# A two-block transformer kernel on one core: order of the first loads, place of the modulation's columns, and layout of SBUF

## The reference

```python
cond = jax.nn.silu(c)
for i in range(DEPTH):                       # 2 layers
    mod = cond @ ada_w[i] + ada_b[i]         # 1024 -> 6 * 1024
    sh1, sc1, g1, sh2, sc2, g2 = jnp.split(mod, 6, axis=-1)
    h = modulate(rms_norm(x, norm_g[i, 0]), sh1, sc1)
    y = nsa_mixer(h, ...) if i == 0 else swa_sink_mixer(h, ...)
    x = x + (1 + g1)[:, None, :] * rms_norm(y, norm_g[i, 1])
    h = modulate(rms_norm(x, norm_g[i, 2]), sh2, sc2)
    y = squared_relu_mlp(h, mlp_w_up[i], mlp_w_down[i])
    x = x + (1 + g2)[:, None, :] * rms_norm(y, norm_g[i, 3])
# in nsa_mixer, keys and values are compressed by a small MLP, "phi":
#   gelu(xb @ w1 + b1) @ w2 + b2,  w1: 2 x (2048 x 256), 2 MB a side
# in the second block: kv = rmsnorm(mem, mem_norm) @ w_mem_kv
```

## Time and profile before

| | |
|---|---|
| times of three runs | 2752.65, 2753.83 (median), 2754.45 us |
| profiled execution | 2753.48 us, its span 2751.7 us |
| granted TensorE clock, mean | 0.962 |
| PE busy | 2563.0 us (93%) |
| POOL busy | 1775.8 us (65%) |
| DVE busy | 1378.4 us (50%) |
| ACT busy | 698.0 us (25%) |
| moved by DMA | 260.13 MB, mean 95 GB/s |

### The profile page before, as it was taken

One profiled execution on the slowest core, in us unless ns is written; L12 is line 12 of the kernel. 1 busy time (PEld: TensorE's weight loads), 2 busy tenths in 40 slices (PEclk: granted clock), 3 DMA queues, 4 the chain that ended last, 5 costly groups with the idle time before them and its releaser, 6 DMA issues. The chain is left out here.

```text
span 2751.7 us, 36593 instructions
## 1 busy us (share of the span) xinstructions
PE 2563.0 (93%) x11854; PEld 2052.2 (75%) x11854; DVE 1378.4 (50%) x2631; ACT 698.0 (25%) x1475; POOL 1775.8 (65%) x983
## 2 busy tenths in 40 slices
PE   7798888899999888899999899999999899999998
PEld 6676666688888667688888587777777776787876
DVE  6378888433442477422112466666128534652552
ACT  3302777211001227211101222232006323100001
POOL 5364444577777567587777444445779867687784
PEclk9898999999999989999999999999999999999999
DMA  7573000254652220233333222212333223233332
GB/s 254 153 214 118 1 1 16 61 178 158 213 176 84 62 62 26 86 98 99 92 98 93 84 62 62 62 54 62 94 103 65 72 61 111 84 94 97 92 103 73
DMA packets 420546, 260.13 MB, mean 95 GB/s; under 512 B 62844, under 2 KB 411513, under 8 KB 414017
## 3 DMA queue, kind: packets, MB, share of 16 engines
q1 hardware_dynamic: 390811, 191.28, 24.2%
q10 hardware_dynamic: 29606, 67.22, 7.2%
HBM read 254.25 MB, written 8.10 MB: 95 GB/s over the span
## 5 line engine op out<-in xcount | busy, mean ns | idle before, releaser
L654 POOL TENSOR_TENSOR W<-RAW,zeros 128x1024 fp32r<-128x1024 f32 (+2 forms) x355 | 680.5, 1917 | 698.7 <-PE PA L735 335.2
L661 POOL TENSOR_TENSOR W<-RAW,W 128x1024 fp32r<-128x1024 f32 (+2 forms) x355 | 851.7, 2399 | 48.2 <-PE PA L741 22.0
L734 PE MATMUL PA<-H,W 128*128 128x512 f32 x1272 | 506.4, 398 | 6.4 <-DVEq L2289 2.3
L735 PE MATMUL PA<-H,W 128*128 128x512 f32 x1272 | 495.6, 390 | 0.0
L734 PE MATMUL PA<-A,W 128*128 128x512 f32 x944 | 381.1, 404 | 16.0 <-DVE A L1921 10.8
L735 PE MATMUL PA<-A,W 128*128 128x512 f32 x944 | 378.5, 401 | 0.0
L741 PE MATMUL PA<-H,W 128*128 128x512 f32 x1272 | 316.3, 390 | 0.0
L734 PEld LDWEIGHTS PA<-H,W 128*128 128x128 f32 x1272 | 238.9, 188 | 64.2 <-POOL W L654 6.9
L735 PEld LDWEIGHTS PA<-H,W 128*128 128x128 f32 x1272 | 238.8, 188 | 54.5 <-issue 5.5
L741 PEld LDWEIGHTS PA<-H,W 128*128 128x128 f32 x1272 | 238.9, 188 | 49.3
L741 PE MATMUL PA<-A,W 128*128 128x512 f32 x944 | 249.7, 402 | 0.0
(11 more groups left out here) (362 smaller groups left out, 3919.2 us busy)
## 6 DMA issues: line engine op xcount, KB each, us to landing
AD<-in_ada_w_dram ACTq DMA_DIRECT2D x40, 1024.0 KB, 5.5
RAW<-in_w_in_dram SPq DMA_DIRECT2D x160, 256.0 KB, 3.1
RAW<-in_mlp_w_up_dram SPq DMA_DIRECT2D x128, 256.0 KB, 3.1
RAW<-in_mlp_w_down_dram SPq DMA_DIRECT2D x128, 256.0 KB, 3.0
RAW<-in_w_up_dram SPq DMA_DIRECT2D x88, 256.0 KB, 3.1
RAW<-in_nsa_w_in_dram SPq DMA_DIRECT2D x40, 256.0 KB, 4.1
RAW<-in_w_down_dram SPq DMA_DIRECT2D x16, 384.0 KB, 3.4
RAW<-in_swa_w_in_dram SPq DMA_DIRECT2D x20, 256.0 KB, 3.3
```

What stands on the lines that cost most here:

```text
L654: e.tensor_tensor(W[0][:, s, 0:kc], RAW[:, s, 0:kc], zeros[:, 0:1].rearrange("p (a b) -> p a b", b=1).broadcast_to([P, kc, P]), ALU.add).t ...
L661: e.tensor_tensor(W[1][:, s, 0:kc], RAW[:, s, 0:kc], W[0][:, s, 0:kc].bitcast(F32), ALU.subtract).then_inc(w_split, 1)
L734: pe.matmul(PA[s][:, 0:n], W[0][:, s, k], hi, start=(k == 0), stop=False)
L735: mm = pe.matmul(PA[s][:, 0:n], W[0][:, s, k], lo, start=False, stop=False)
```

## The change

Four things change, and no arithmetic does.

1. SP's queue no longer begins with the 13 row tiles, and ACT's no longer holds ada pieces 0 to 3. SP now has RAW for panels 0 and 1, x, ada 0 and 1, RAW for 2 and 3, ada 2 to 5, RAW for 4, ada 6 and 7 (`ADA_BEHIND`). The row tiles are issued by ACT behind constants, mem and positions. DVE's wait for the positions moves into `angle(0)`, and each `angle` comes one copy later.
2. PHI1's two sides, one DMA each, are issued by ACT apart (`phi_load`): side 0 after the inverse root of x and a wait for six ada pieces, side 1 in the middle of writing H. `columns(0)` on PE moves ahead of the wait for the inverse, and the last two value turns use alternate banks, without a wait of their own for the copy before.
3. `column_pairs` becomes `single_columns`: one column matmul behind each of the sixteen W0 matmuls of the panel (the last of them behind the wait for `w_split`), the eight W1 matmuls then follow without any.
4. The order of allocation becomes RAW, W0, W1, H0 and H1 (ADAH, KEPT), the region of PHI1, ADA and A0, then A1, MH0, MH1, and only then X (GATE), Y, the constants and tmp tiles. KM and all behind it keep their place.

```diff
@@ allocations @@
-    X = sb("X", [P, DC, S])
+    RAW = sb("RAW", [P, 2, GC, P])
+    W = [sb(f"W{i}", [P, 2, GC, P], F32R) for i in range(2)]
     H = [sb(f"H{i}", [P, DC, S], F32R) for i in range(2)]
-    Y = sb("Y", [P, DC, S])
-    RAW = sb("RAW", [P, 2, GC, P])
-    W = [sb(f"W{i}", [P, 2, GC, P], F32R) for i in range(2)]
-    cst = sb("cst", [P, sum(w for _, w in off.values())])
...
     A = [sb(f"A{i}", [P, GC, S], F32R) for i in range(2)]
...
+    X = sb("X", [P, DC, S])
+    Y = sb("Y", [P, DC, S])
+    cst = sb("cst", [P, sum(w for _, w in off.values())])
...
+    ADA_BEHIND = {1: (0, 1), 3: (2, 3, 4, 5), 4: (6, 7)}
...
             if isinstance(p, int) and p == 1:
                 sp.dma_start(OT[:], T["x"].rearrange("a (b p) n -> p (a b) n", p=P)).then_inc(sem("loaded_x"), 16)
-            if isinstance(p, int) and p == 3:
-                for m in range(4, DC):
+            if isinstance(p, int) and p in ADA_BEHIND:
+                for m in ADA_BEHIND[p]:
                     e.dma_start(ADA_FIRST[m], ada_piece(m)).then_inc(sem(f"ada_first{m}"), 16)
 
-        for r in range(4):
-            for src, row in c_tiles[r]:
-                sp.dma_start(KM[row:row + src.shape[0], r, 0:P], src).then_inc(sem("loaded_rows"), 16)
...
                 pe.matmul(PA[s][:, 0:n], W[0][:, s, k], hi, start=(k == 0), stop=False)
+                if between:
+                    between(2 * k)
                 mm = pe.matmul(PA[s][:, 0:n], W[0][:, s, k], lo, start=False, stop=False)
+                if between and k < kc - 1:
+                    between(2 * k + 1)
             mm.then_inc(w_hi_used, 1)
             pe.wait_ge(w_split, p + 1)
+            if between:
+                between(2 * kc - 1)
             for k in range(kc):
-                if between:
-                    between(k)
...
-        def column_pairs(n):
-
-            def pair(k):
-                if k == 0:
+        def single_columns(n):
+
+            def one(j):
+                if j == 0:
                     pe.wait_ge(sem("mod_acc"), DC * (n + 1))
-                column(2 * k)
-                mm = column(2 * k + 1)
-                if k == DC - 1:
+                mm = column(j)
+                if j == 2 * DC - 1:
                     mm.then_inc(sem("mod_cols"), 1)
...
             pe.wait_ge(panel_free, 5 + k)
-            pe.wait_ge(sem("turned_taken"), c["turned"])
-            transposes([tmp[4 + k % 2][:, b * P:b * P + P] for b in range(2)], bank=PT[1])
+            if k < 2:
+                pe.wait_ge(sem("turned_taken"), c["turned"])
+            transposes([tmp[4 + k % 2][:, b * P:b * P + P] for b in range(2)], bank=PT[1 if k < 2 else k % 2])
...
         panels(2, [(DC, None)], MH, 256)
+        columns(0)
         pe.wait_ge(sem("inverse"), 2)
         mem_value_turn(0)
-        columns(0)
...
-        for m in range(4):
-            aux(ADA_FIRST[m], ada_piece(m), f"ada_first{m}")
+        for r in range(4):
+            for src, row in c_tiles[r]:
+                aux(KM[row:row + src.shape[0], r, 0:P], src, "loaded_rows")
...
+        def phi_load(side):
+            aux(PHI1[:, side], T["nsa_phi_w1"][0, side].rearrange("(l q) n -> q l n", q=P), "phi_loaded")
...
         inverse_root(PT[0], PT[0], S, "inverse")
+        act.wait_ge(sem("mod_acc"), 6)
+        phi_load(0)
         mem_value_copy(0)
...
         mem_value_copy(3)
+        phi_load(1)
         round_hi(H, DC - 3, lambda k: mod(0, 0)(k + 3), at=3)
...
-        act.wait_ge(panel_ready, 8)
-        for side in range(2):
-            aux(PHI1[:, side], T["nsa_phi_w1"][0, side].rearrange("(l q) n -> q l n", q=P), "phi_loaded")
```

More of the change, by code:

```diff
@@ L114, in sem @@
         return sems[name]
-    with ExitStack() as over:
-        GATE = sb("GATE", [P, DC, S], F32, over)
-    X = sb("X", [P, DC, S])
-    x_spill = nc.dram_tensor("x_spill", (P, DC, S), F32, kind="Internal").ap()
+    RAW = sb("RAW", [P, 2, GC, P])
+    W = [sb(f"W{i}", [P, 2, GC, P], F32R) for i in range(2)]
     with ExitStack() as over:
@@ L125, in build @@
     H = [sb(f"H{i}", [P, DC, S], F32R) for i in range(2)]
-    Y = sb("Y", [P, DC, S])
-    RAW = sb("RAW", [P, 2, GC, P])
-    W = [sb(f"W{i}", [P, 2, GC, P], F32R) for i in range(2)]
-    cst = sb("cst", [P, sum(w for _, w in off.values())])
-    cols = sb("cols", [P, 4, P])
-    modT = sb("modT", [P, 2, 48])
-    coefA = sb("coefA", [P, 2, 4, DC])
-    zeros = sb("zeros", [P, 1])
-    cosT = sb("cosT", [P, S])
-    sinT = sb("sinT", [P, S])
-    tmp = [sb(f"tmp{i}", [P, S]) for i in range(2)]
-    with ExitStack() as over:
-        TURN0 = sb("TURN0", [P, 4, S], F32R, over)
-    tmp += [sb(f"tmp{i}", [P, S]) for i in range(2, 6)]
-    small = sb("small", [P, 16])
-    sinks = sb("sinks", [P, 2, 16])
-    roots = sb("roots", [P, 8])
-    peak4, sum4 = (sb(f"{n}4", [P, 2, NT]) for n in ("peak", "sum"))
-    stat = [sb(f"stat_{n}", [P, 8]) for n in ("neg", "four", "sum", "inv")]
-    inverse4 = stat[1][:].rearrange("p (a n) -> p a n", a=2)
     with ExitStack() as over:
@@ L176, in build @@
     A = [sb(f"A{i}", [P, GC, S], F32R) for i in range(2)]
+    with ExitStack() as over:
+        GATE = sb("GATE", [P, DC, S], F32, over)
+    X = sb("X", [P, DC, S])
+    x_spill = nc.dram_tensor("x_spill", (P, DC, S), F32, kind="Internal").ap()
+    Y = sb("Y", [P, DC, S])
+    cst = sb("cst", [P, sum(w for _, w in off.values())])
+    cols = sb("cols", [P, 4, P])
+    modT = sb("modT", [P, 2, 48])
+    coefA = sb("coefA", [P, 2, 4, DC])
+    zeros = sb("zeros", [P, 1])
+    cosT = sb("cosT", [P, S])
+    sinT = sb("sinT", [P, S])
+    tmp = [sb(f"tmp{i}", [P, S]) for i in range(2)]
+    with ExitStack() as over:
+        TURN0 = sb("TURN0", [P, 4, S], F32R, over)
+    tmp += [sb(f"tmp{i}", [P, S]) for i in range(2, 6)]
+    small = sb("small", [P, 16])
+    sinks = sb("sinks", [P, 2, 16])
+    roots = sb("roots", [P, 8])
+    peak4, sum4 = (sb(f"{n}4", [P, 2, NT]) for n in ("peak", "sum"))
+    stat = [sb(f"stat_{n}", [P, 8]) for n in ("neg", "four", "sum", "inv")]
+    inverse4 = stat[1][:].rearrange("p (a n) -> p a n", a=2)
     KM = sb("KM", [P, 4, 256])
@@ L999, in mlp @@
                 panel_mm(p, p % 2, DC, A, need=lambda k: pe.wait_ge(panel_free, p - 8 + k + 1),
-                         between=column_pairs(2 + g) if ada and g else None)
+                         between=single_columns(2 + g) if ada and g else None)
                 c["panel"] += 1
@@ L1012, in columns @@
             mm.then_inc(sem("mod_cols"), 1)
-        def column_pairs(n):
-            def pair(k):
-                if k == 0:
+        def single_columns(n):
+            def one(j):
+                if j == 0:
                     pe.wait_ge(sem("mod_acc"), DC * (n + 1))
-                column(2 * k)
-                mm = column(2 * k + 1)
-                if k == DC - 1:
+                mm = column(j)
+                if j == 2 * DC - 1:
                     mm.then_inc(sem("mod_cols"), 1)
-            return pair
+            return one
         def mem_turn(k):
@@ L1129, in _ @@
         hidden(1, 1)
-        project([rotate] * 4 + [turn] * 4 + [rotate], H, first=lambda: compressed(1), between=column_pairs(1))
+        project([rotate] * 4 + [turn] * 4 + [rotate], H, first=lambda: compressed(1), between=single_columns(1))
         project([rotate] * 7 + [turn], H)
@@ L1454, in mem_value_take @@
             act.wait_ge(sem("turned"), 20 + k + 1)
-            act.activation(VM[:, :, k * P:k * P + P], PT[1][:, 0:256].rearrange("p (b n) -> p b n", b=2), ACT.Copy).then_inc(sem("turned_taken"), 1)
+            act.activation(VM[:, :, k * P:k * P + P], PT[1 if k < 2 else k % 2][:, 0:256].rearrange("p (b n) -> p b n", b=2), ACT.Copy).then_inc(sem("turned_taken"), 1)
         for k in range(DC):
```

6 lines of the change are left out of this document (4 added, 2 removed).

## The result

The changed kernel takes 2719.91 us in the median of four runs (2717.22 to 2723.41), the kernel before, beside it, 2753.24: 0.9891 of it, 95% interval 0.9876 to 0.9906. That is 33.3 us less where 44.7 were forecast; the range of 2700 to 2731 us holds it, the likeliest case's own bounds of 2702 to 2716 do not. The profiled execution took 2720.13 us (span 2718.3), 33.35 less than the one of before.

The account below looks back on a forecast made before the run. The prediction took PE, busy 93% of the span, as the bound. A's pitch −18.4, columns −11.3 and prologue −15.0 sum to −44.7 us, from 2753.8 to 2709 us; range 2700 to 2731.

Parts of the forecast that it names:

- the likeliest case: Whole kernel: layout, columns and prologue all give their gains, 2709 us, own bounds 2702 to 2716; chance 0.50.
- The term of 18.4 us: A panels: tiles placed low, or starting on a multiple of 64 bytes, bring A matmuls to H's pitch, −18.4 us.
- The columns: Four column panels: single columns spread among the first sixteen matmuls hold the clock, 3 x 3.1 + 2.0 = −11.3 us.
- 5.44 and two turns of 0.5 together: NSA column panel: its cost without columns; 11.58 us is 5.6 over it, 3.6 columns and 2.0 clock.
- The prologue: Start up to the hidden layer: reordered loads and PE work start that layer at 99.2, not 114.16, −15.0 us.
- (a): Prologue, first memory pair: RAW first on SP lets the pair end at 29.9 instead of 37.06, −7.1 us.
- (b): Prologue, columns(0) moved ahead of two waits: columns run from 51.8, first H pair starts at 67.8, −7.9 us.
- (d): Prologue, ACT's queue: big phi weight loads leave the place between small loads and table load, −4.6 us.
- One: A panels: the place yields nothing, the 6.67 ns belong to A's use; 2727 us, chance 0.17.
- Two: Column panels: the clock falls in the spread columns too; 2720 us, chance 0.12.
- Four: H and A panels: pitch hangs on something else in the layout, H gets 233.3 ns, A keeps it; 2761 us, chance 0.04.
- Three: Prologue gives half, as early loads delay mem and x, or projection weights come late; 2716 us, chance 0.10.

Follow-up runs that it names:

- the six layouts: Kernel before, changed kernel, and four that move 32 to 96 bytes of small tiles across A's region in either: 2742.61, 2734.36, 2721.41 and 2739.57 us.
- the second trace: The changed kernel, unaltered, run again beside the kernel with small loads and PHI1 loads later: 2720.56 us, ratio 0.9893 to the kernel before.
- the one with the later loads: Changed kernel with phi's small loads and then both PHI1 loads issued right after the rotation tables: 2713.75 us, ratio 0.9885; again 2715.80, 0.9880.

## Why the prediction held, and where it was off

**A's pitch: right, and the reason was one of the two named.** The term of 18.4 us can be checked on the trace as what remains. Before minus after is 6.3 us at the hidden layer, 0.9 in the NSA column panel, 238.8 − 235.0 = 3.8 in the attention stage, 3 x 3.1 in the MLP column panels beside A's pitch, and −5.3 where runs of A panels end (below); 33.35 − 6.3 − 0.9 − 3.8 − 9.3 + 5.3 leaves 18.4, in which single steps of the clock of 1 to 1.5 us either way are still contained, so that it is the forecast number to the tenth is luck. Counted directly, over the 2638 steps from one A matmul to the next that ran at the upper clock in both traces, it is 17.1 us, or 6.5 ns a step; by that the term was right within a tenth. The formula of the Trainium skill in which the gap depends on the columns alone (TensorE: Matmul & The Clock Gate, "Back-to-back issue gap") would have made it 0; the six layouts show 226.7 to 233.3 ns for the same 512 columns. In the prediction H's tiles were called the sign of what "a low and even place" does; low had no part in it.

**The columns: right for three panels, mis-sized for the fourth.** The MLP panels gave 3.1 us each, as reckoned (the prediction says that the three panels show the same two numbers; they are 11.16 and 6.78, 10.74 and 7.19, 10.33 and 7.60, and only the sums agree, 17.93 to 17.94). Beside the new layout the fall itself is cheaper, 3.2 + 1.6 + 1.6 = 6.4 us in the experiment with the layout alone, so this term and A's were costed as independent and are not quite. A column alone costs what half a pair did: the panel is 9.09 us, 24 x 0.2267 + 16 x 0.228. The NSA panel fell from 11.58 to 10.70 us (its neighbours' starts are 175.16 and 185.86), 0.9 and not 2.0. The step "5.44 and two turns of 0.5 together" left out what follows this panel in the changed kernel too:

```profile
185.30 1.12 PE L836 MATMUL PT<-tmp,cst 128*128 128x512 f32 x2 [0.35 <-DVE tmp L1730]
```

It is a rotation, two 512-column fp32 matmuls that are in every panel of that kind (such a panel takes 6.35 us, 0.9 over 5.44), and ahead of it PE waits 0.35 us for DVE's copy. Neither is a loss of clock. The next panel gives another 0.3 us (6.22 and 5.90), so 1.2 us came of the columns there in all.

**The prologue: 6.3 us at the hidden layer, not 15.0.** The prediction called itself wrong "if the hidden layer starts after 105". It starts at 107.84, and at 105.84 in the second trace, so by its own sign this part was wrong. (a) was right to 0.3 us: the memory pair ends at 30.19. (b) was right up to columns(0), 52.43 against 51.8, and wrong for the H pair: "they are now issued 30 us and more earlier" was costed as pure gain. A load that is moved earlier is moved beside other loads. The weights of panel 7 took 6.3 us in place of 3.0, POOL lost 3.5 us, and the pair started at 72.02: 4.2 us late. With PHI1 late it starts at 69.06, so 3.0 of the 4.2 are this load's; the other 1.2 are not accounted for. The prediction had read in the profile that RAW's packets starve beside longer ones (14.4 us to land) and used it only where it helped. (d) lost the other 4.4: from the H pair to the hidden layer it took 38.5 us before, 31.4 by the prediction, 35.8 now. DVE's sums started as early as reckoned, relative to the pair, but the steps themselves are slower. These two rows are of before, where POOL had nothing to do from 102.70 to 106.80 us:

```profile
102.58 0.69 DVE L2071 TENSOR_TENSOR OT<-OT,PE 128x512 f32<-128x512 f32 x1 [8.60 <-ACT OT L1509]
...
105.96 0.69 DVE L1733 TENSOR_TENSOR KC<-KC,tmp 128x512 f32<-128x512 f32 x1
```

After, POOL splits from 93.21 to 102.95 us, and the same sums take 2.37 and 2.76 us, two of the four steps behind them 1.77 and 1.99. Together that is 1.68 + 2.07 + 1.09 + 1.30 = 6.1 us more, less the 1.5 that the step of 2.21 no longer loses: 4.6. The prediction allowed for that one slow step to become fast and for none to become slow. In the second trace, where the first sum came ahead of POOL's split, it took 33.6 us from the pair to the hidden layer, so (d) lost 2.2 us there and 4.4 here: half of it hangs on how the steps happen to meet. The Trainium skill has the rule for such meetings (SBUF — State Buffer, "Who interferes with whom": a VectorE step with two inputs in SBUF contends with a GpSimd step that reads SBUF, by an exclusive lock on shared ports), and the rows agree: 0.69 us alone, 1.8 to 2.8 here beside POOL, while the step at 100.78, one of whose two inputs is in PSUM, took 0.69 beside it. The first sums also waited 3.27 us for the sinks load, one of the small loads that the prediction gave "14 us to land"; moved earlier, with PHI1 late, the small loads were worth 3.5 us.

**What was not in the sum.** Where a run of A panels ends, PE waits for the residual, and there the changed kernel is slower. The end of the first MLP, before and after (from the last A panel's start to the first H panel behind the pair):

```profile
913.50:951.90 38.40, 30.27 (x95) 17.01 (x94) 23.21 (x34) 14.24 (x22) 13.02 (x9) 0.91 0.14 31
```

```profile
886.80:927.00 40.20, 32.18 (x94) 20.08 (x94) 23.20 (x34) 14.24 (x22) 13.11 (x9) 0.83 0.14 32
```

The same work takes 40.2 us in place of 38.4, with the clock at 0.83 in place of 0.91; two later ends of such runs lose 1.5 and 2.0. DVE's, ACT's and POOL's busy times are equal to 0.1 us, PE's is 1.9 longer, so it is the clock. The mean clock says the same of the whole: 0.962 of 2751.7 us leaves 2 x 0.038 x 2751.7 = 209 us at the lower level, 0.964 of 2718.3 leaves 196. The column panels alone gave up 2 x 24 x (0.14 x 3 + 0.07) = 23.5 us of it, so some 10 us came back elsewhere. What decides in which of its pauses PE loses the clock was not tried. In part it goes with A's pitch. From the last A matmul at the last of these three ends to the last of the 48 H panels behind it, seven of the eight traces with A at 5.44 us take 430.0 to 430.1 us, high place or low, the eighth 427.7, and the six with a slower A 427.7 to 428.4. In part it is the single run: at the end of the first MLP two traces of one kernel, the one with the later loads, differ by 1.8 us.

**The total.** It fell short by 44.7 − 33.35 = 11.3 us: 8.7 in the prologue, 1.1 in the NSA column panel, and 5.3 − 3.8 = 1.5 in stages that were not in the sum. That these last two nearly cancel is luck, and the 3.8 stands beside the 2.4 by which one kernel's own traces differ there.

**Rivals.** One (the place yields nothing) is refuted by the pitch. Two (the clock falls in the spread columns) by the windows. Four (H takes the slow pitch) too. Three, "the prologue gives half", is what happened, but by neither of its reasons: mem and x were on time, and the late weights were not the projection's but those of the last memory panels, behind a load that the change itself had moved. It was given 0.10. The time named for rival two, 2720, is the measured one, and its mechanism is the one that the traces refute: a total doesn't tell causes apart.

## What to carry to other kernels

Start the moving tiles of matmuls on a multiple of 128 bytes: moving 96 bytes of small tiles is enough for the pitch, and on a kernel bound by PE most of it goes into the time. Where small matmuls have to be mixed into a dense stream, try them one by one, and early in the panel, and look at the granted clock. A load that is moved ahead of its need is free only where the queues are empty: look up what else is landing there, above all loads with shorter packets on which another engine waits. And before a stage is read from one trace, look at how far two traces of one kernel differ in it.
